# Sixteen shifted copies instead of 128 in the bias round trip of a transformer layer, read back in eight loads

## The reference, cut to what matters

```python
def rel_bias_grid(table, dist):
    b = jnp.take(table, t5_bucket(dist), axis=0)
    return jnp.moveaxis(b, -1, 0).reshape(N_NSA_KV, NSA_GROUP, *dist.shape)

s = jnp.einsum('bgrqd,bgkd->bgrqk', qb, kb) * scale + rel_bias_grid(table, dist)
p = masked_softmax(s, valid)
```

## Time and profile before

| | us |
|---|---|
| median of 3 runs | 1889.43 |
| lowest, highest | 1888.48, 1889.85 |
| profiled execution | 1888.83 |
| its span, first to last instruction | 1887.1 |
| mean granted TensorE clock | 0.833 of full |

### The profile page before, as it was taken

The page is one execution under the profiler, slowest core; times in us unless marked ns, Lnnn a source line. Parts: engine busy times, 40 slices in busy tenths (PEclk is TensorE's granted clock), DMA queues, the critical chain, the costliest instruction groups (busy, mean ns, idle before and its releaser), DMA issues.

```text
span 1887.1 us, 12624 instructions
## 1 busy us (share of the span) xinstructions
PE 1282.0 (68%) x3739; PEld 691.2 (37%) x3739; DVE 1343.8 (71%) x1811; ACT 377.1 (20%) x642; POOL 807.5 (43%) x539
## 2 busy tenths in 40 slices
PE   4799999989866667656555555655565555555567
PEld 3688887777644434211111111111121111111122
DVE  3354556355559989787787877878787787878764
ACT  3233442443422121111110101011011110101001
POOL 1000010000003655665665656666655666665654
PEclk8899999989888889877877778777777777777779
DMA  7666644415429999999999999999999999999998
GB/s 171 196 190 189 186 138 127 142 61 207 156 88 406 413 421 418 421 421 422 421 422 422 417 421 405 419 417 420 421 413 411 422 414 422 419 407 422 422 422 355
DMA packets 129230, 636.22 MB, mean 337 GB/s; under 512 B 13762, under 2 KB 22564, under 8 KB 63124
## 3 DMA queue, kind: packets, MB, share of 16 engines
q0 software_dynamic: 75136, 540.58, 70.0%
q1 hardware_dynamic: 54036, 94.95, 15.4%
HBM read 631.29 MB, written 4.19 MB: 337 GB/s over the span
## 4 chain that ended last, share of the span: by engine, by line
DMA 43%; PE 33%; DVE 8%; POOL 7%; issue 6%; ACT 2%; POOLq 0%; SPq 0%; DVEq 0%; ACTq 0%
DMA big<-in_peer_expert_v,pick_row 27%; DMA big<-in_peer_expert_u,pick_row 13%; PE ps L1443 11%; PE ps L1159 6%; PE ps L1160 6%; PE ps L1161 6%; POOL big L420 5%; DVE big L1078 3%; DMA raw<-in_w_in 2%; POOL big L415 2%; DVE split_lo L647 1%; PE ps L1226 1%; DMA raw<-in_peer_w_query 1%; PE ps L1146 1%; DVE ht L675 1%
## 5 line engine op out<-in xcount | busy, mean ns | idle before, releaser
L1443 PE MATMUL ps<-big,diag 128*128 128x512 f32 x1024 | 706.1, 828 | 491.2 <-DMA big<-in_peer_expert_v,pick_row 439.4
L1078 DVE CUSTOM_DVE_ANT_0 big<-big 128x2048 f32<-128x2048 f32 x256 | 586.2, 2291 | 212.1 <-DMA big<-in_peer_expert_u,pick_row 210.8
L420 POOL DMA_INDIRECT big<-in_peer_expert_v,pick_row x256 | 448.1, 1751 | 391.1 <-PE ps L1443 291.2
L1443 PEld LDWEIGHTS ps<-big,diag 128*128 128x128 f32 x1024 | 225.9, 243 | 960.1 <-DMA big<-in_peer_expert_v,pick_row 716.3
L415 POOL DMA_INDIRECT big<-in_peer_expert_u,pick_row x256 | 339.8, 1327 | 180.7 <-issue 70.4
L1096 DVE SCALAR_TENSOR_TENSOR big<-big,pick_w 128x1024 f32<-128x1024 f32 x256 | 327.5, 1279 | 47.8 <-DMA big<-in_peer_expert_v,pick_row 46.4
L647 DVE TENSOR_TENSOR split_lo<-raw,split_hi 128x1024 fp32r<-128x1024 f32 x152 | 185.7, 1223 | 197.8 <-ACT split_hi L444 167.6
L1159 PE MATMUL ps<-split_hi,ht 128*128 128x512 f32 x608 | 248.4, 409 | 73.9 <-DVE split_lo L647 73.9
L610 ACT ACTIVATE diag<-ident,pick_w 128x128 f32<-128x128 f32 x256 | 95.3, 395 | 808.0 <-PE ps L1443 489.1
L1160 PE MATMUL ps<-split_lo,ht 128*128 128x512 f32 x608 | 241.6, 397 | 0.0
L1161 PE MATMUL ps<-split_hi,ht 128*128 128x512 f32 x608 | 241.2, 397 | 0.0
(11 more groups left out here) (193 smaller groups left out, 677.2 us busy)
## 6 DMA issues: line engine op xcount, KB each, us to landing
raw<-in_w_in SPq DMA_DIRECT2D x88, 512.0 KB, 4.6
raw<-in_w_out SPq DMA_DIRECT2D x32, 512.0 KB, 3.5
raw<-in_peer_w_query SPq DMA_DIRECT2D x32, 512.0 KB, 11.1
raw<-in_cmp_k_w SPq DMA_DIRECT2D x8, 512.0 KB, 4.0
raw<-in_cmp_v_w SPq DMA_DIRECT2D x8, 512.0 KB, 4.1
big<-in_peer_expert_u,pick_row POOLq DMA_INDIRECT x256, 11.5
big<-in_peer_expert_v,pick_row POOLq DMA_INDIRECT x256, 11.4
big<-in_x SPq DMA_DIRECT2D x2, 1024.0 KB, 5.9
```

The source lines that it names most:

```text
L420: pool.indirect_dma_start(ring[g % RING], None, v_table, bass.IndirectOffsetOnAxis(pick_row[:, m - LAG:m - LAG + 1], 0)).then_inc(gathered ...
L1078: dve.tensor_tensor_reduce(row, row, XN[:, m // (PICKS // TT), :], 1.0, 0.0, ALU.mult, ALU.add, pick_dot[:, m:m + 1]).then_inc(dotted, 1)
L1443: ins = pe.matmul(psf[:, t * V_PE + c:t * V_PE + c + 512], diag[:, m % DIAGS, :], row[:, c:c + 512], start=k == 0, stop=k == PICKS // TT - 1)
```

## The change

`bias_dram` holds 16 copies for each head instead of 128. The store writes these 16. The load is cut into eight: load b fills partitions 16 b to 16 b + 15, reads the same 16 shifted copies, and starts 16 b numbers further to the left. Before each load POOL waits until weight step 12 + 4 b has been split (`split_done`). DVE's wait counts all eight loads.

```diff
 BIAS_W = 512
+SHIFTS = 16
+BIAS_AFTER, BIAS_APART = 12, 4
...
-        bias_dram = nc.dram_tensor("bias_dram", [NH, P, BIAS_W + 1], F32, kind="Internal").ap()
+        bias_dram = nc.dram_tensor("bias_dram", [NH, SHIFTS, BIAS_W + 1], F32, kind="Internal").ap()
...
             pool.wait_ge(sem("bias_rows"), 1)
-            pool.dma_start(bias_dram[:, :, 0:BIAS_W], ROWB.unsqueeze(1).broadcast_to([NH, P, BIAS_W])).then_inc(sem("bias_stored"), 16)
+            pool.dma_start(bias_dram[:, :, 0:BIAS_W], ROWB.unsqueeze(1).broadcast_to([NH, SHIFTS, BIAS_W])).then_inc(sem("bias_stored"), 16)
             pool.wait_ge(sem("bias_stored"), 16)
-            pool.dma_start(BIAS, bass.AP(tensor=bias_dram.tensor, offset=P, ap=[[BIAS_W, P], [P * (BIAS_W + 1), NH], [1, 384]])).then_inc(sem("bias_loaded"), 16)
+            for b in range(P // SHIFTS):
+                pool.wait_ge(split_done, SP_IN + BIAS_AFTER + BIAS_APART * b)
+                pool.dma_start(BIAS[b * SHIFTS:(b + 1) * SHIFTS],
+                               bass.AP(tensor=bias_dram.tensor, offset=P - b * SHIFTS,
+                                       ap=[[BIAS_W, SHIFTS], [SHIFTS * (BIAS_W + 1), NH], [1, 384]])).then_inc(sem("bias_loaded"), 16)
...
-                    dve.wait_ge(sem("bias_loaded"), 16)
+                    dve.wait_ge(sem("bias_loaded"), 16 * (P // SHIFTS))
                     sb_out(0)
```

## The result

| | before | after |
|---|---|---|
| median, us | 1888.95 (4 runs) | 1860.2 (4 runs) |
| lowest, highest | 1886.16, 1889.85 | 1857.29, 1861.74 |
| profiled execution | 1888.83 | 1861.74 |
| its span | 1887.1 | 1860.0 |

The ratio is 0.9848, with a 95% interval of 0.9831 to 0.9866: the change takes 28.75 us off the median. Forecast were 28.1 us and 1861.3; measured is 1860.2. One run of the kernel before was added beside the three shown earlier.

What follows compares the result with a forecast made beforehand. Weight loads held beside the bias store were taken to delay the first 70 us. Gain 28.1 us, less 0 for the bias loads and 0 for the waits, takes the median from 1889.43 to 1861.3 us; range 1857.5 to 1866.5.

Steps and rivals of the forecast that it cites:

- The hole: ACT's copies of weight steps 5 to 7 wait for weight loads beside the store; removing the waits gains 28.1 us.
- The store: POOL's bias store, 2048 KB cut to 256 KB: lands after 5.8 us by bytes, 9.2 at most, instead of 46.0.
- if the delay scales with the store: Step 5's weight load, issued at 20.5 us: its 27.3 us shrink by 8, landing at 23.9, wanted at 30.97.
- My other bound, behind the store: Step 5's weight load behind a store lasting to 25.8 us: lands near 29 to 30.4 us, still in time.
- rival (b): No change: the store stays some 40 us long, or something else delays the weights; 1886 to 1890 us, chance 0.03.
- The eight loads: Bias loads of 192 KB beside the weight stream, about 50 to 126 us: cost taken as 0, 4.0 us at most.
- the slack of 3.8 us: Spare time of a weight load in the steady stretch: 8.4 us of lead less 4.6 us to land.
- the old load's place: The single 1536 KB bias load at 63 to 73 us: cost nothing there, so moving it gives nothing.
- POOL's and DVE's waits: POOL's eight issues, at most 7.7 us, have some 85 us of cover; DVE's wait precedes line 781's copy; both cost nothing.
- What is late next: After the early wait TensorE's beat paces; low-clock drops in later stretches may shift the time 3 to 4 us either way.
- (a): The bias loads or remaining store cost part of the gain: 1865.3 us, or 1868 with a late first step; chance 0.10.
- (c): Slower: each bias load stops weights long, steps 12 to 44, 7.8 us hold each; 1894 us and above, chance 0.02.

## Why the prediction was right, and where its steps were off

**The hole.** Right. Steps 5, 6 and 7 were late because of the store: 128 copies with the new loads give 1888.7, no round trip at all gives 1860.8. The sum of 28.1 us, from ACT's rows, is what step 10 (44.63 against 44.6 forecast) and POOL's power (215.78 against 215.8) show. The median moved by 28.75 and the profiled execution by 27.1; that these lie so close about 28.1 is in part luck, as the low clock behind the hole moves a time by some 3 us.

**The store.** It landed after 7.8 us, between 5.8 (in proportion) and 9.2 (my upper bound). The outcome held, but the step "if the delay scales with the store" did not: in proportion to the copies, 27.3 us become 6.8 for 32 copies and 13.7 for 64, and 10.5 and 20.7 were measured. What holds up to 64 copies is that the weight load behind the store lands 0.7 to 1.7 us after it; with 128 it lands 15 us before the store's end, which is why a proportion from that row misled. My other bound, behind the store, was the right kind. So the margin in rival (b), "it may last about 17 us", was wrong; by the runs it is about 13 us of landing time, since 13.1 us is just late. The changed kernel's 7.8 leaves 5.

**The eight loads.** Hidden, as forecast, with the time of no round trip. The size I took for the hold, 0.4 us each from the row of the old load, was too small. Bunched, the loads take 2.1 us each, near the 2.2 us that I had from the store and set aside. Spaced, a weight load lands after up to 5.9 us, where it takes 3.5 with no bias load near: a hold of up to 2.4 us, hidden by the slack of 3.8 us and not by being small. I called the spacing free; I had not seen that it is needed. Without it 8 to 10 us of the gain are lost. I had taken the hold of a load as independent of its neighbours. The sentence that the old load's place cost nothing stands, but for a load of 128 partitions only.

**POOL's and DVE's waits.** Right: 88.59 us of cover on POOL, the copy behind DVE's wait starts at 238.54 (238.6 forecast).

**What is late next.** Right in kind: the gather forecast near 535 came at 538.4 and at 534.8 in two executions, for the most part by the low clock, as allowed for with 3 to 4 us.

**The rivals.** (a) did not happen at this spacing and does at others: one load for each step gives 1864.75, near its 1865.3, but that number was made from a hold of 4.3 us a load, so the match is luck. (b) is excluded by the runs. (c) did not happen; even three times the loads stay 17 us below the kernel before, though a landing then reaches 12.9 us, over the 12.4 that (c) asked for at each of the eight.

## What to carry to other kernels

A slow background transfer beside a stream of loads can do its harm by who is served first and not by bytes: here 90 GB/s moved while TensorE stood still, against 196 in the steady stretch. Look in the chain for a load of the stream that takes far longer than its like, and see which queue's transfer is in flight meanwhile. Cut that transfer until it ends before the next load is due (here 256 KB hid entirely, 512 KB just showed, 1024 KB cost 14 us), or read it from more partitions, which alone gave 18 to 19 of the 28 us. If narrow transfers take the place of a wide one, space them against the beat of the stream, and measure the spacing: here one for every second beat was free, one for every beat cost 5 to 6 us, all at once 8 to 10. Whether the 16 copies could be read back by one load of all 128 partitions was not tried.

## What was not expected of the hardware

- The same 2048 KB store from eight neighbouring partitions, from eight that lie four apart, and from 128: 46.0, 24.2 and 19.2 us.
- The fastest of these stores was no better for the kernel than the middle one (1869.9 and 1869.3 us), since its queue was the only one that moved anything from 20 to 30 us: 17.0 us for a weight load of 512 KB.
- In 22 to 36 us of the kernel before, the weights' packets came to half of each of the three loads issued up to 27.9 us; later the two queues went one for one. Why the order changes is open.
- A weight load behind the store lands just after it for stores of 256, 512 and 1024 KB, and 15 us before the end of one of 2048 KB.
- In the steady stretch a weight load lands after 4.6 us in the kernel before and after 3.5 us in the changed one from 135 to 200 us (3.6 without the round trip), at the same beat. It costs nothing here, and its cause was not looked for.
